# Six unused products behind the ninth product of a slab, in three stretches of a three-layer block on one core

## The reference

```python
def sqrelu_mlp(hn, w1, w2):                       # D_FF = 4096, used in both first layers
    return jnp.square(jax.nn.relu(hn @ w1)) @ w2
...
x = x + sqrelu_mlp(rms_norm(x, norm_mlp[i]), mlp_w1[i], mlp_w2[i])
...
up = jnp.einsum("bsd,df->bsf", h, w_up[layer])    # second part, 2 * D_FF_2 = 6144 columns
up = causal_dwconv(up, conv_f_w[layer], conv_f_b[layer])
gate, val = jnp.split(up, 2, axis=-1)
ffn_out = jnp.einsum("bsf,fd->bsd", jax.nn.gelu(gate) * val, w_down[layer])
```

## Time and profile before

| | |
|---|---|
| runs | 1194.15, 1190.89, 1200.25 us; median 1194.15 |
| profiled execution | 1196.76 us |
| its span | 1195.0 us, mean granted TensorE clock 0.981 |
| products on TensorE | 9437, each with a weight load |
| slab products with moving activations `act`, per pass | 1640, mean 282 to 285 ns |
| with moving activations `hid`, per pass | 512, mean 281 ns |
| traffic | 192.67 MB, mean 161 GB/s |

### The profile page before, as it was taken

The page is one execution under the profiler, slowest core; times in us unless marked ns, Lnnn a source line. Parts: engine busy times, 40 slices in busy tenths (PEclk is TensorE's granted clock), DMA queues, the critical chain, the costliest instruction groups (busy, mean ns, idle before and its releaser), DMA issues.

```text
span 1195.0 us, 21698 instructions
## 1 busy us (share of the span) xinstructions
PE 1144.5 (96%) x9437; PEld 1104.4 (92%) x9437; DVE 792.3 (66%) x1131; ACT 588.3 (49%) x825; POOL 130.6 (11%) x84
## 2 busy tenths in 40 slices
PE   6899899999999999999999999999999979999997
PEld 5898789999998898999999889999988879999997
DVE  5647658775436665877544888777465778888742
ACT  4257854444344555544333465655255546665531
POOL 3000040000220003100022302400000030101000
PEclk8699999999999999999999999999999989999999
DMA  9733135655554444556556471556444535556550
GB/s 274 218 106 120 58 116 178 198 180 182 197 186 142 154 134 138 177 181 197 187 177 188 114 223 36 185 169 201 136 124 142 165 117 177 181 195 207 177 177 36
DMA packets 194723, 192.67 MB, mean 161 GB/s; under 512 B 9675, under 2 KB 192692, under 8 KB 194628
## 3 DMA queue, kind: packets, MB, share of 16 engines
q1 hardware_dynamic: 191360, 188.43, 49.8%
q10 hardware_dynamic: 3268, 2.84, 1.0%
HBM read 189.78 MB, written 1.47 MB: 160 GB/s over the span
## 4 chain that ended last, share of the span: by engine, by line
PE 84%; DVE 8%; ACT 3%; issue 2%; ACTq 1%; POOL 1%; DVEq 0%
PE ps_gemm L1576 75%; DVE w_lo L1036 2%; PE ps_score L1643 2%; PE ps_out L1676 2%; PE ps_trans L1661 2%; PE ps_score L1871 2%; DVE xc L1347 1%; PE ps_gemm L1747 1%; ACTq L789 1%; DVE rs L1048 1%; ACTq L776 1%; DVE h_rnn L1386 0%; POOL rg_t L657 0%; PE ps_score L1649 0%; DVE act_lo L1042 0%
## 5 line engine op out<-in xcount | busy, mean ns | idle before, releaser
L1576 PE MATMUL ps_gemm<-act_hi,w_hi 128*128 128x256 f32 x1640 | 464.2, 285 | 22.8 <-ACT act_hi L970 6.7
L1576 PE MATMUL ps_gemm<-act_hi,w_lo 128*128 128x256 f32 x1640 | 459.5, 282 | 0.0
L1576 PE MATMUL ps_gemm<-act_lo,w_hi 128*128 128x256 f32 x1640 | 448.1, 282 | 0.0
L1036 DVE TENSOR_TENSOR w_lo<-raw,w_hi 128x2048 fp32r<-128x2048 f32 (+2 forms) x179 | 407.3, 2283 | 42.8 <-ACT w_hi L694 42.4
L694 ACT ACTIVATE w_hi<-raw 128x2048 fp32r<-128x2048 f32 (+2 forms) x179 | 332.5, 1862 | 175.4 <-DMA raw<-in_mlp_w 96.0
L1576 PEld LDWEIGHTS ps_gemm<-act_hi,w_hi 128*128 128x128 f32 x1640 | 312.3, 190 | 28.1 <-issue 15.7
L1576 PEld LDWEIGHTS ps_gemm<-act_hi,w_lo 128*128 128x128 f32 x1640 | 314.8, 192 | 0.2
L1576 PEld LDWEIGHTS ps_gemm<-act_lo,w_hi 128*128 128x128 f32 x1640 | 304.6, 189 | 1.5
L1576 PE MATMUL ps_gemm<-hid_hi,w_hi 128*128 128x256 f32 x512 | 143.9, 281 | 0.0
L1576 PE MATMUL ps_gemm<-hid_lo,w_hi 128*128 128x256 f32 x512 | 143.9, 281 | 0.0
L1576 PE MATMUL ps_gemm<-hid_hi,w_lo 128*128 128x256 f32 x512 | 143.9, 281 | 0.0
(11 more groups left out here) (305 smaller groups left out, 1691.8 us busy)
## 6 DMA issues: line engine op xcount, KB each, us to landing
raw<-in_mlp_w SPq DMA_DIRECT2D x64, 1024.0 KB, 5.2
raw<-in_w_in SPq DMA_DIRECT2D x30, 1024.0 KB, 5.4
raw<-in_w_up SPq DMA_DIRECT2D x24, 1024.0 KB, 5.2
raw<-in_od_w_in SPq DMA_DIRECT2D x12, 1024.0 KB, 5.1
raw<-in_w_down SPq DMA_DIRECT2D x12, 1024.0 KB, 5.1
raw<-in_ev_w_in SPq DMA_DIRECT2D x9, 1024.0 KB, 6.9
raw<-in_w_proj_a SPq DMA_DIRECT2D x8, 640.0 KB, 4.1
raw<-in_ev_w_out SPq DMA_DIRECT2D x4, 1024.0 KB, 5.2
```

Source lines behind the costliest of these rows:

```text
L1036: dve.tensor_tensor(w_lo[:, slot, 0:k, 0:n], raw[:, slot, 0:k, 0:n], w_hi[:, slot, 0:k, 0:n].bitcast(F32), ALU.subtract).then_inc(w_ready, 1)
L1576: ins = pe.matmul(dst, lhs, rhs, start=(first and opens and i == 0), stop=(last and closes and i + 1 == len(order)), skip_group_check=True)
```

## The change

`gemm` gets a parameter `lock`. With it, ahead of the product with index 9 of the slab (k = 1, second half, first pass), that is behind the ninth, six products are issued with the slab's weights moving and 128 tokens of the activations stationary: the passes 0, 1, 2, 0, 1, 2, all of chunk k, each starting and closing its own sum, all into the same 256 columns of `ps_trans`. Nobody reads the result. The parameter is set for slab 1 of `a_up`, `m_up` (through `mlp`) and `f_up`.

```diff
         def gemm(s, g, x_hi, x_lo, kc0=0, n_k=KS, first=True, last=True, tok_major=False, n=NS, m=None,
-                 before_pair=None, before_chunk=None, low_last=False, between=None, ks=None, opens=True, closes=True):
+                 before_pair=None, before_chunk=None, low_last=False, between=None, ks=None, opens=True, closes=True,
+                 lock=False):
...
                 w, xx = passes[q]
+                if lock and i == 9:
+                    for r in range(6):
+                        wr, xr = passes[r % 3]
+                        pe.matmul(ps_t[:, 0, 0:NS], xr[:, kc0 + k, 0:P], wr[:, slot, k, :], start=True, stop=True)
                 if tok_major:
...
             for j in range(16):
-                gemm(s0 + j, g0 + j, act_hi, act_lo, before_chunk=x_in(n) if j == 0 else None, low_last=j == 0)
+                gemm(s0 + j, g0 + j, act_hi, act_lo, before_chunk=x_in(n) if j == 0 else None, low_last=j == 0,
+                     lock=j == 1)
...
         for j in range(24):
-            gemm(s0 + j, g0 + j, act_hi, act_lo, before_chunk=x_in(6) if j == 0 else None, low_last=j == 0)
+            gemm(s0 + j, g0 + j, act_hi, act_lo, before_chunk=x_in(6) if j == 0 else None, low_last=j == 0,
+                 lock=j == 1)
```

## The result

| | before | after |
|---|---|---|
| runs | 22 | 22 |
| median | 1195.18 us (1185.76 to 1202.83) | 1200.37 us (1195.89 to 1202.47) |
| ratio | | 1.0048, 95% interval 1.0029 to 1.0068 |
| profiled execution, its span | 1196.76, 1195.0 us | 1201.14, 1199.3 us |

The kernel became 5.2 us slower. Forecast were 2.1 us more, 1196.3, in a range that ended at 1200. The result is within the 1% that the prediction took for no change, but the whole interval of the ratio lies above 1, and the median is just above the range. Worth noting from the start: the slowest runs of the two kernels are alike (1202.8 and 1202.5); the fastest are 10 us apart. What the change took away are the low times.

The account below looks back on a forecast made before the run. TensorE, busy 96%, was taken as bound by its product pace. 2 x (0.68 + 39 x 0.0046 - 0.15) + 0.71 = +2.1 us on the median 1194.15 gave 1196.3 us; range 1176 to 1200, the forecast's own 1192 to 1200.

Parts of the forecast that it names:

- Slow was forecast for all three: Behind the six products in a_up, m_up and f_up, products run at 117.8 ns, not about 113.3; chance 0.36.
- The price of 0.71 us each: Net cost per stretch: MLPs 0.68 for six products, plus 39 x 0.0046, less 0.15; f_up 0.71 for six products.
- The bank wait: At slab 2 of both MLPs, TensorE's first product waits for a bank freed by VectorE's `up_r`; forecast to go.
- the term of -0.15: Gain of 0.15 us in each MLP stretch from the vanished wait at slab 2.
- slab 3 brought no new one: Slab 3's `w_lo` and bank, the next possible wait in the MLPs, were forecast to be ready in time, costing nothing.
- Rivals 1 to 3: Quick stretches: all three, 1177.0 us (chance 0.30); only the two MLPs, 1182.7 (0.11); only f_up, 1190.5 (0.12).
- The reason for the third stretch: f_up stays slow: its stream has the 280 ns pass at `w_lo`, like the one that stayed slow at 402.5.
- the base of the sum: Whole kernel: +2.1 us, worked out on the profiled 1196.76 us execution, was added to the median shown, 1194.15.
- only the 39 are quick now: In each MLP stretch, of 1479 products behind the six, only slab 1's remaining 39 run quick before the change.
- Rival 4: Stages behind the stretches: some 730 quick products fall slow, losing 3.4 us, giving 1199.7; chance 0.10.
- up to 2.0 more: Last 432 products, behind the 16 transposes: up to 2.0 us further gain if they too turn quick.

Follow-up runs that it names:

- the insertion twice: Against the kernel before, six products with moving weights inserted twice, ahead of indexes 9 and 21 of slab 1, in all three stretches: 1187.4 us, ratio 0.9972.
- five products: Against the kernel before, five products with moving weights in place of six, inserted in f_up alone: 1191.22 us, ratio 0.9960.
- f_up-only trace: Against the kernel before, the insertion of six in f_up alone, MLPs untouched: 1194.85 us, ratio 0.9983.
- MLPs-only one: Against the kernel before, the insertion of six in the two MLPs alone, f_up untouched: 1201.91 us, ratio 1.0051.

## Why the prediction missed

**The outcome in each stretch was right.** Slow was forecast for all three, and all three are slow. The price of 0.71 us each is 0.74, 0.72 and 0.70 in the profiled pair. The first of these is in part luck: the stream came in slow there and not quick as forecast; the second, which came in quick, is the test of the sum. The bank wait vanished, as the term of -0.15 said, and slab 3 brought no new one. The granted clock, VectorE and the transfers played no part. Rivals 1 to 3, with quick stretches, did not occur with this kernel, though each of them is a kernel one line away.

**The reason for the third stretch was the right one, on thin ground.** From a mean of 280 against 279 ns the prediction took it that a slow stream whose marked pass is the third stays slow and one in which it is the first turns quick. Six products (stays slow), the insertion twice (second border turns quick), five products (turns quick) and the 42 borders of the kernels' own bear it out.

**The step that failed is the base of the sum.** The prediction says: "it lies 2.6 us above the median shown, 1194.15, so I predict 1194.15 + 2.1". That carries a price worked out for one execution, with both MLPs slow, over to a median of executions that aren't all like it. The line before it, "of which only the 39 are quick now", is true of the profiled execution and false of the kernel. In the five traces with untouched MLPs, 5 of 10 MLP stretches are quick behind slab 2 (both in two traces, none in two, one of the two in the fifth), and each is worth 6.39 us (181.48 - 175.09). The changed kernel had both slow in its trace, as had the kernel with the insertions in the MLPs alone, and that loss isn't in the sum. The forecast was 4.1 us short: 3.1 by the price of the change (5.2 in place of 2.1), and 1.0 because the median of three runs, 1194.15, became 1195.18 with 22.

What belongs there: against a trace with all three stretches in the slow rhythm the change costs 2.16 us in them and gives 1.91 back in f_dn, 0.25 in all. The rest of the 5.2 us, 4.9, would be 0.8 of a quick stretch per execution out of two, some 40%. That share is an inference from the medians; the 5 of 10 in the traces fit it, but are too few to give a share, and the stages outside the stretches vary by some us as well. That the MLPs are the place is shown by the insertions in them alone, which make the whole loss, and the scatter (17.1 us before, 6.6 after) and the slowest runs being equal fit it.

**It could have been seen.** The three runs of before span 9.4 us, and the prediction noted that this "is also about one long stretch's 6.6 us in another rhythm", but used it only for the width of the range. Taken as a mixture, it says: a forecast "all stretches slow whatever comes in" is a forecast of the time at the upper end, near 1200.25. The measured median is 1200.37; that it meets the highest of three runs so closely is chance.

**Rival 4**, slower by the stages behind, was half there and is not the cause. The 144 products of the earlier trace rows did turn slow, +0.62 us of the 3.4 it priced. (The 730 products behind that price aren't the sum of the rows named there: 144 and 312 make 456, and the other quick row lies in the first stretch. The trace of before has 720 products between 735.8 and 821.5 us, quick for the most part.) But they have 16.97 us in the f_up-only trace, where nothing ahead of them is changed, and 16.35 in the MLPs-only one. They vary by themselves.

**The f_dn tail** was bounded ("up to 2.0 more") but only for the case that f_up goes quick. It went the other way round: f_up slow in another phase made the tail quick, and f_up quick left it slow. Here too the phase ahead counted, not only the rhythm.

On the rule weighed in the prediction: the Trainium skill, "TensorE: Matmul & The Clock Gate", Part 2 (step 1), says that streaming and weight loading have read ports of their own; it says nothing of operand roles. That neither rhythm nor role would matter was the prediction's own conclusion from it, and that doesn't hold in these streams: the same six products have a ratio of 1.0048 with the weights moving and of 0.9971 with the activations moving.

**What stays open.** Why a border acts so, and what in the chip makes one load of three 4 ns longer and three steps together 13.5 ns longer (3 x 117.8 against 3 x 113.3): the traces show durations and starts, and no cause was tried. What the bank wait draws by: in the five traces with untouched MLPs nine stretches came to it quick, five left it quick (steps of 0.19 to 0.20 us into and behind the first product) and four slow (0.18 to 0.20), so the length of the wait doesn't tell them apart. Why the share of quick executions differs between chips, and how often the streams enter slab 1 slow: of the 28 MLP stretches in all 14 traces, 24 came in quick and 4 slow, third, ahead of anything inserted. And why the insertion of six twice scatters by 13.2 us and that of three twice by 3.4.

## What to carry to other kernels

Ahead of any sum, ask whether the kernel's own runs are one population: a scatter of 1% with one stretch worth 0.5% in another rhythm can be a mixture, a second trace of the same kernel can show it, and a change that fixes the outcome of a draw must be priced against the mixture, not against the one profiled execution. In long streams of products, look at the distance between starts and at which pass has the longer loads; both are to be had from one trace and told in this kernel what the next border would do. And a fixed rhythm is worth having for the scatter alone: a few products of swapped roles, in a number chosen by the phase that comes in, held this kernel near its fastest (1182.08 to 1186.54 us in ten runs, where the kernel before had 1186.71 to 1203.25).

## What the runs showed of the hardware

- A stream of products with their weight loads, 256 columns each, runs at 113.3 or 117.8 ns a product at a granted clock of 1.00, with the same instructions, and stays so over 1500 products and all slab borders without a wait.
- In the slow rhythm one pass of three has weight loads of 192 ns beside 188. Which of the three it is is a state of its own, carried along for hundreds of products.
- A border from moving weights back to moving activations, with three or more products of moving weights ahead of it, turned quick to slow first, slow third to slow first, and slow first to quick, in every insertion traced here; the 42 borders of the kernels' own did the same, and slow second to quick. The border the other way kept quick, slow first and slow third; slow second came out as slow first (the insertions twice of six and of three, at 791.6 and 794.6 us).
- The sixteen transposes inside f_dn set the rhythm by the phase ahead of them in the same way in all traces: behind a quick f_up the 432 products took 50.89 us, behind a slow third one 50.90, behind a slow first one 48.98.
